# One stage for rotation, local attention and the decays of linear attention

## The chip, the core and the metric

The kernel runs on one core of a Trainium2 chip. The metric is the device time of one execution in microseconds. The core has TensorE (PE, matmuls into PSUM), VectorE (DVE), ScalarE (ACT), GpSimd (POOL) and SyncE (SP, here only the issue of DMAs); each has its own queue of instructions, and they wait for each other on semaphores. Everything is float32.

## What is computed

The reference is a trunk of two layers over 512 latent and 256 context tokens (768 rows, T) of width 1024. Layer 0 has a gated linear attention (GLA, 4 heads) beside a local attention (8 query heads, 2 key heads, window 128), layer 1 a latent attention; each layer ends in a mixture of 64 experts. Of layer 0 this matters:

```python
def apply_rope(x, ang):
    cos, sin = jnp.cos(a), jnp.sin(a)
    x1, x2 = xf[..., :half], xf[..., half:]
    return jnp.concatenate([x1 * cos - x2 * sin, x2 * cos + x1 * sin], axis=-1)

def gla_log_decay(a_low, wa2, ba):
    return jax.nn.log_sigmoid((a_low @ wa2 + ba).astype(jnp.float32)) / GLA_TAU
...
    cum = jnp.cumsum(ac, axis=2)                      # of the log decays, in a chunk
    o = einsum(qc * jnp.exp(cum), state) + ...
    state = jnp.exp(last)[..., None] * state + einsum(kc * jnp.exp(last - cum), vc)
...
    a_l = swa_latent(apply_rope(lsq, ang), apply_rope(lsk, ang), lsv, csk, csv, sink)
```

Latent queries and keys of the local attention are rotated, those of the context are not. A latent block of 128 queries sees all 256 context keys and the latent blocks beside it; a context block sees the context alone.

## The kernel before

Layer 0 is a row of stages (class `Phase`), each with its own buffers and semaphores and closed by a barrier of all engines. In order: `norm_transpose`, `even_project` (projections, with the modulation weights streamed through `wm` buffers), `rotate` (line 847), `window_attention` (line 894), `gla_decays` (line 516), `gla_states` (line 650), `gla_outputs`, `mix_out`, and the experts. Nothing reorders instructions: each engine runs its part of a stage as the code is written.

`rotate` turns six 128 x 512 tiles (four of queries `sqT`, two of keys `skT`). PE multiplies a tile by the constant `swap` (L871), DVE multiplies the result by the sines (L887), POOL the tile itself by the cosines (L878), DVE adds them (L891).

`window_attention` goes over six query tiles t of 128 rows (0 and 1 are context) and eight heads. PE writes the scores of one head to one of two `raw` buffers (L957 context keys, L959 near keys); DVE adds the mask and takes the maximum (L1017); after eight heads `maxima` gives the bias (L1023 to L1027); ACT takes the exponentials (L1072, L1076). PE turns them in quads of four heads and one key block (L969), DVE and ACT copy the even and the odd quads to `pT` (L1034, L1085), PE multiplies with the values (L981), ACT copies the result (L1091), PE turns it back (L991), DVE divides (L1039 to L1046). A loop over `steps(t)` (8, 8, 10, 12, 12 and 10 steps) pairs the scores of head i of tile t + 1 with quad i - 2 of tile t, the same on PE and DVE. Keys per tile: 2, 2, 4, 5, 5, 4 blocks, so scores are 256 wide for tiles 0 and 1, 512 for 2, 640 for 3 and 4, 512 for 5. "Tile t" below means step loop t, in which the scores of t + 1 are made.

`gla_decays` works on four 128 x 768 rows x of `qa` and `kb` (two directions, two pairs of heads). PE makes the logits in eight PSUM buffers (L551); ACT Abs (L628), Exp (L632), Ln (L635); DVE the other part of the log sigmoid (L567), the difference (L573), the cumulative sum (L575), the reversal for the backward direction (L580 to L586), the centring on the middle of each chunk (L590), the carries (L597, L602) and the scaled queries (L607); ACT the factors (L638, L640) and the carry factors (L646); POOL zeroes half of `qb` and `sm` (L614, L615) and multiplies the keys (L619). SP loads the small weights `wa` and `ba` once DVE has cleared `wa`.

`gla_states` issues the load of `w_out_e` (L1136), turns keys, and DVE runs the states from one chunk to the next. It does not wait for the zeroing within the stage.

## Time and profile before

| | us |
|---|---|
| median of 3 timed runs | 2854.18 |
| lowest, highest | 2849.14, 2856.47 |
| profiled execution | 2864.24 |
| its span, first to last instruction | 2861.7 |
| mean granted clock of PE | 0.930 |

The profile is one execution. Its times are from the span's start. "Busy" leaves out waiting; the granted clock is 1.00 at 2.4 GHz and 0.50 at 1.2 GHz. A bracket behind an instruction gives the engine's idle time before it and what ended it.

### The profile page before, as it was taken

The page shows a single profiled execution, that of the slowest core. Times are in us where ns is not written, and L with a number is a line of the kernel's source. Part 1 is how long each engine was busy: PE and PEld are TensorE (multiplying, and loading weights), DVE is VectorE, ACT ScalarE, POOL GpSimd, SP SyncE. Part 2 cuts the span into 40 slices and gives each one's busy share as a digit, 9 for nine tenths or more (in the row PEclk, how much of TensorE's full clock was granted, in tenths as well). Part 3 has the DMA queues.
Part 4 walks back from the last instruction along what each step waited for, and adds up shares of the span by engine and source line. Part 5 has one row for each costly group of instructions (what it writes and reads, how often), then busy time and mean ns, then how long its engine had stood idle before and what let it go on. Part 6 is the DMA issues. An engine that isn't in the chain of part 4 may idle for free. (4 is left out here: it accounts for less than half of the span.)

```text
span 2861.7 us, 30812 instructions
## 1 busy us (share of the span) xinstructions
PE 2522.1 (88%) x9117; PEld 1161.8 (41%) x9118; DVE 1200.0 (42%) x2435; ACT 410.1 (14%) x867; POOL 857.6 (30%) x1012
## 2 busy tenths in 40 slices
PE   6999794595599999999995998999389999999996
PEld 2665352452333333333332543554233333333332
DVE  2997255724633233332349112332533233332327
ACT  2000144221000000000014111222000000000002
POOL 0111102101354545545413001000054545545432
PEclk8999796797799999999998997999689999999998
DMA  7756000210599999999965201001479988998866
GB/s 255 226 191 220 19 1 1 65 67 32 223 369 365 361 348 361 350 364 364 363 266 228 66 30 67 1 1 44 178 252 355 345 324 331 338 337 336 331 221 272
DMA packets 163887, 634.31 MB, mean 222 GB/s; under 512 B 51710, under 2 KB 58282, under 8 KB 113506
## 3 DMA queue, kind: packets, MB, share of 16 engines
q10 hardware_dynamic: 59984, 389.57, 36.8%
q0 software_dynamic: 55280, 129.67, 12.4%
q1 hardware_dynamic: 48548, 114.13, 10.7%
q8 instruction: 39, 0.64, 0.1%
q14 instruction: 36, 0.29, 0.0%
HBM read 609.96 MB, written 74.58 MB: 239 GB/s over the span
## 5 line engine op out<-in xcount | busy, mean ns | idle before, releaser
L1759 POOL DMA_INDIRECT xg<-rows_x,p_idx x520 | 530.6, 1020 | 231.9 <-issue 122.0
L1847 PE MATMUL p_gu<-ring,p_xT 128*128 128x512 f32 x1024 | 455.7, 598 | 26.4 <-DVE p_xT L2088 26.4
L1859 PE MATMUL p_gu<-ring,p_xT 128*64 x1024 | 453.2, 595 | 0.0
L1860 PE MATMUL p_gu<-ring,p_xT 128*64 128x512 f32 x1024 | 453.1, 595 | 0.0
L2094 DVE TENSOR_TENSOR p_hid<-p_gu,p_sg 128x256 f32<-128x256 f32 x128 | 54.4, 425 | 580.8 <-ACT p_sg L1972 580.8
L1847 PEld LDWEIGHTS p_gu<-ring,p_xT 128*128 128x128 f32 x1024 | 192.0, 193 | 244.5 <-issue 244.5
L2088 DVE STREAM_TRANSPOSE p_xT<-xg 128x1024 f32<-128x1024 f32 x130 | 263.7, 2028 | 28.8 <-DMA xg<-rows_x,p_idx 27.1
L1859 PEld LDWEIGHTS p_gu<-ring,p_xT 128*64 128x64 f32 x1024 | 135.0, 137 | 263.9 <-issue 256.2
L2104 DVE COPY p_ys<-p_y 128x512 f32<-128x512 f32 x128 | 88.5, 692 | 365.6 <-PE p_y L1888 184.8
L1886 PE MATMUL p_y<-ring,p_hT 128*64 x512 | 233.4, 599 | 5.1 <-issue 5.1
L1875 PE MATMUL p_y<-ring,p_hT 128*128 128x512 f32 x512 | 236.9, 606 | 0.0
L1888 PE MATMUL p_y<-ring,p_hT 128*64 128x512 f32 x512 | 233.4, 598 | 0.0
L1972 ACT ACTIVATE p_sg<-p_gu 128x256 f32<-128x256 f32 x128 | 49.0, 383 | 877.9 <-PE p_gu L1860 439.6
L1773 POOL DMA_INDIRECT rows_y<-p_ys,p_y_idx x128 | 132.1, 1032 | 112.8 <-POOL p_y_idx L1770 111.9
L1875 PEld LDWEIGHTS p_y<-ring,p_hT 128*128 128x128 f32 x512 | 92.0, 189 | 143.8 <-issue 143.8
L1978 ACT COPY p_ys<-p_y 128x512 f32<-128x512 f32 x128 | 74.9, 585 | 424.6 <-PE p_y L1875 211.8
L1860 PEld LDWEIGHTS p_gu<-ring,p_xT 128*64 128x64 f32 x1024 | 135.0, 137 | 0.0
L1300 POOL TENSOR_TENSOR p_row<-p_tmp,p_mod_b 128x1024 f32<-128x1024 f32 x10 | 23.5, 2348 | 367.8 <-DVE p_tmp L1285 367.8
L1886 PEld LDWEIGHTS p_y<-ring,p_hT 128*64 128x64 f32 x512 | 64.8, 136 | 162.0 <-issue 162.0
L1770 POOL COPY p_y_idx<-slot_pair 128x1 int32 (+1 forms) x128 | 23.9, 186 | 348.5 <-DVE p_ys L2104 317.6
L453 PE MATMUL p_bank<-uT_e,w_in_e 128*128 128x384 f32 (+1 forms) x352 | 121.1, 500 | 2.3 <-PEq L111 2.3
L484 DVE SCALAR_TENSOR_TENSOR p_part<-p_wm,silu_c,p_part 128x256 f32<-128x256 f32 x273 | 111.3, 478 | 0.0
(424 smaller groups left out, 3066.8 us busy)
## 6 DMA issues: line engine op xcount, KB each, us to landing
ring<-in_w_exp_gate ACTq DMA_DIRECT2D x120, 1024.0 KB
ring<-in_w_exp_up ACTq DMA_DIRECT2D x120, 1024.0 KB
ring<-in_w_exp_down ACTq DMA_DIRECT2D x120, 1024.0 KB
ring<-rows_y SPq DMA_DIRECT2D x80, 512.0 KB, 12.8
p_wm<-in_w_mod POOLq DMA_DIRECT2D x24, 1024.0 KB
cat_e<-in_w_mod POOLq DMA_DIRECT2D x16, 1024.0 KB, 6.2
xg<-rows_x,p_idx POOLq DMA_INDIRECT x520
p_wmod<-in_w_mod SPq DMA_DIRECT2D x4, 2048.0 KB, 19.7
```

What stands on the lines that cost most here:

```text
L453: mm = nc.tensor.matmul(o, lhs, rhs, start=(k == 0), stop=(k == KD - 1))
L484: ins = nc.vector.scalar_tensor_tensor(acc, wm[sl % MBUF][:, k, :], c, acc, ALU.mult, ALU.add)
L1759: nc.gpsimd.indirect_dma_start(out=xg[q][:, part * D // QUADS:(part + 1) * D // QUADS], out_offset=None, in_=tr.rows_x[:, :].rearrange("t ...
L1773: nc.gpsimd.indirect_dma_start(out=tr.rows_y[:, :], out_offset=bass.IndirectOffsetOnAxis(ap=y_idx[q][:, 0:1], axis=0), in_=ys[q][:], in_of ...
L1847: mm = nc.tensor.matmul(gu[q][:], xT[q][:, k, :], w[:, :, k, :], start=(k == 0), stop=(k == KD - 1))
L1859: nc.tensor.matmul(gu[q][lower, :], xT[q][:, k, lower], wa[:, :, k, :], start=first, stop=last)
L1860: mm = nc.tensor.matmul(gu[q][upper, :], xT[q][:, k, upper], wb[:, :, k, :], start=first, stop=last)
L1875: mm = nc.tensor.matmul(yb[half], hT[q][:, k, :], w[:, k, half * 512:(half + 1) * 512], start=(k == 0), stop=(k == 1))
L1886: nc.tensor.matmul(yb[half][lower, :], hT[q][:, k, lower], wa[:, k, cols], start=(k == 0), stop=(k == 1))
L1888: mm = nc.tensor.matmul(yb[half][upper, :], hT[q][:, k, upper], wb[:, k, cols], start=(k == 0), stop=(k == 1))
L2088: nc.vector.transpose(xT[q][:].rearrange("p k (q b) -> p q k b", q=QUADS), xg[q][:].rearrange("p (q f k) -> p q k f", q=QUADS, k=KD)).then ...
L2104: nc.vector.tensor_copy(ys[q][:, 0:512], yb[0]).then_inc(y_v, 1)
```

## The change

Three stages become one, `local_attention`. `rotate` stays for layer 1 only, `gla_decays` is gone, its buffers `qa`, `kb` and `carry` are allocated earlier and lent to `even_project` as `wm` buffers. The context tiles need no rotation: the scores of tile 0 are made first, then come the six swaps and the four pairs of logits on PE, which uses the PSUM buffers of attention (`turn`, `ot`, `op` for the swaps, the two `raw` for the logits, each in turn). Abs and the splits follow them on ACT and DVE. Exp and Ln of the decays stand in ACT's queue after tile 0, differences and cumulative sums in DVE's steps 2 and 5 of tiles 1 and 2, the reversal and the centring in tile 3, the carries in tile 4, the scaled queries in tile 5; the factors stand in ACT's queue after tiles 3 and 4. The zeroing of `qb` and `sm` moves to `gla_states`.

```diff
         product, read_dve, read_act = ph.sem("product"), ph.sem("read_dve"), ph.sem("read_act")
-        wm = [ph.sb(f"wm{i}", [P, KD, MC])[:] for i in range(MBUF - 2)]
+        wm = [decays[:, i * KD * MC:(i + 1) * KD * MC].rearrange("p (k n) -> p k n", n=MC) for i in range(MBUF - 2)]
         wm += [spare[:, 2 * i:2 * i + 2, :].rearrange("p t (k n) -> p (t k) n", n=MC) for i in range(2)]
...
-def gla_decays(tr, qkT, aT, qa, kb, carry, qb, sm):
...
-    with Phase(nc) as ph:
-        wa = ph.sb("wa", [2 * GRANK, 2, GH * GDK])
-        ba = ph.sb("ba", [P, 4])
-        reset = ph.sb("reset", [P, T])
-        mid, total = ph.sb("mid", [P, 4, NT]), ph.sb("total", [P, 4, NT])
-        low = [ph.ps(f"low{i}", [P, 512]) for i in range(8)]
...
@@ -661,6 +527,13 @@
             @block.sync
             def _(sp):
                 load_ahead(sp)
+            @block.gpsimd
+            def _(pool):
+                for i in range(2):
+                    other = slice((1 - i) * GDK, (2 - i) * GDK)
+                    nc.gpsimd.memset(qb[other, :, :, i, :], 0.0)
+                    nc.gpsimd.memset(sm[other, :, :, i, :], 0.0)
             @block.tensor
             def _(pe):
...
-def window_attention(tr, sqT, skT, sv, cat):
+def local_attention(tr, sqT, skT, sv, cat, qkT, aT, qa, kb, carry):
...
+        wa = cat[0:2 * GRANK, 4, 0:2 * GH * GDK].rearrange("p (d n) -> p d n", d=2)
+        rope, part = cat[:, 0:2, 0:NLAT], cat[:, 2:4, 0:NLAT]
+        swap, ba = ph.sb("swap", [P, P]), ph.sb("ba", [P, 4])
+        reset = pT[:, CT + 2].rearrange("p h n -> p (h n)")[:, 0:T]
+        mid, whole = ph.sb("mid", [P, 4, NT]), ph.sb("whole", [P, 4, NT])
+        swaps = [turn[0][:].rearrange("p i n -> p (i n)"), turn[1][:].rearrange("p i n -> p (i n)"),
+                 ot[:].rearrange("p i n -> p (i n)"), op[:].rearrange("p i g e -> p (i g e)")]
...
     def _(sp):
         sp.dma_start(mask[:], dr["c_band"]).then_inc(loaded, 16)
         sp.dma_start(sink[:], dr["swa_sink"].to_broadcast([P, SH])).then_inc(loaded, 16)
+        sp.dma_start(swap[:], dr["c_swap"]).then_inc(rope_loaded, 16)
+        sp.dma_start(rope, dr["c_rope"]).then_inc(rope_loaded, 16)
+        sp.wait_ge(cleared, 1)
+        for d in range(2):
+            sp.dma_start(wa[d * GRANK:(d + 1) * GRANK, d, :], dr["gla_wa2"][0, d]).then_inc(wa_loaded, 16)
+            sp.dma_start(ba[:, 2 * d:2 * d + 2], dr["gla_ba"][0, d].rearrange("(j p) -> p j", p=P),
+                         allow_slow_non_contiguous=True) \
+                .then_inc(wa_loaded, 16)
+    @block.gpsimd
+    def _(pool):
+        pool.wait_ge(rope_loaded, 32)
+        for n, x in enumerate(rotating):
+            pool.wait_ge(swapped, n + 1)
+            nc.gpsimd.tensor_tensor(x, x, rope[:, 0, :], ALU.mult).then_inc(cosines, 1)
+        for x in range(4):
+            pool.wait_ge(factor_k, x + 1)
+            nc.gpsimd.tensor_tensor(kb[:, x, :], kb[:, x, :], qkT[:, 2 + x % 2, :], ALU.mult)
...
             n = t * SH + head
             if n >= 2:
                 pe.wait_ge(masked, n - 1)
+            if t == 1 and head < 2:
+                pe.wait_ge(split, 6 + 2 * head)
+                pe.wait_ge(absed, 6 + 2 * head)
+            if t == CT and head == 0:
+                pe.wait_ge(rotated, len(rotating))
...
+        def swap_halves():
+            pe.wait_ge(rope_loaded, 32)
+            for n, x in enumerate(rotating):
+                if n >= 4:
+                    pe.wait_ge(sines, n - 3)
+                nc.tensor.matmul(swaps[n % 4], swap[:], x, start=True, stop=True).then_inc(swapped, 1)
+        def decay_logits(x):
+            if x >= 2:
+                pe.wait_ge(split, 2 * (x - 1))
+                pe.wait_ge(absed, 2 * (x - 1))
+            else:
+                pe.wait_ge(masked, SH - 1 + x)
+            for hf in range(2):
+                mm = nc.tensor.matmul(raw[x % 2][:, hf * 512:hf * 512 + HALF],
+                                      wa[:, x // 2, (x % 2) * P:(x % 2 + 1) * P],
+                                      aT[:, hf * HALF:(hf + 1) * HALF], start=True, stop=True)
+            mm.then_inc(logits, 1)
         def turn_quad(n):
             t, b, q = quads[n]
             pe.wait_ge(probs, SH * t + 4 * (q + 1))
-            if n >= 2:
+            if n < 2:
+                pe.wait_ge(sines, len(rotating))
+            else:
                 pe.wait_ge((placed_v, placed_a)[n % 2], n // 2)
...
         for head in range(SH):
             score(0, head)
+        swap_halves()
+        pe.wait_ge(wa_loaded, 64)
+        for x in range(4):
+            decay_logits(x)
...
     def _(dve):
+        nc.vector.memset(wa, 0.0).then_inc(cleared, 1)
+        nc.vector.memset(reset, 1.0).then_inc(cleared, 1)
+        dve.wait_ge(cleared, 2)
+        nc.vector.memset(reset[:, 0:T:P], 0.0).then_inc(cleared, 1)
         dve.wait_ge(loaded, 32)
+        def turn_halves():
+            dve.wait_ge(rope_loaded, 32)
+            for n, x in enumerate(rotating):
+                dve.wait_ge(swapped, n + 1)
+                if n >= 2:
+                    dve.wait_ge(rotated, n - 1)
+                nc.vector.tensor_tensor(part[:, n % 2, :], swaps[n % 4], rope[:, 1, :], ALU.mult) \
+                    .then_inc(sines, 1)
+                if n:
+                    add_cosines(n - 1)
+            add_cosines(len(rotating) - 1)
+        def add_cosines(n):
+            x = rotating[n]
+            dve.wait_ge(sines, n + 1)
+            dve.wait_ge(cosines, n + 1)
+            nc.vector.tensor_tensor(x, x, part[:, n % 2, :], ALU.add).then_inc(rotated, 1)
+        def split_logits(x):
+            dve.wait_ge(absed, 2 * x + 2)
+            for hf in range(2):
+                nc.vector.tensor_scalar(kb[:, x, hf * HALF:(hf + 1) * HALF], raw[x % 2][:, hf * 512:hf * 512 + HALF],
+                                        ba[:, x:x + 1], 0.0, ALU.add, ALU.min).then_inc(split, 1)
+        def sum_decays(x):
+            dve.wait_ge(logged, x + 1)
+            dve.wait_ge(split, 2 * x + 2)
+            nc.vector.tensor_tensor(kb[:, x, :], kb[:, x, :], qa[:, x, :], ALU.subtract).then_inc(decay, 1)
+            dve.wait_ge(decay, x + 1)
+            dve.wait_ge(cleared, 3)
+            nc.vector.tensor_tensor_scan(qa[:, x, :], reset, kb[:, x, :], 0.0, ALU.mult, ALU.add) \
+                .then_inc(cum_done, 1)
+        def turn_round():
+            dve.wait_ge(cum_done, 4)
+            nc.vector.tensor_copy(whole[:], cum[:, :, :, P - 1]).then_inc(mids, 1)
+            nc.vector.tensor_copy(mid[:, 0:2, :], cum[:, 0:2, :, MID]).then_inc(mids, 1)
+            nc.vector.tensor_tensor(kb[:, 2:4, :], kb[:, 2:4, :], qa[:, 2:4, :], ALU.subtract) \
+                .then_inc(relative, 1)
+            dve.wait_ge(relative, 1)
+            nc.vector.tensor_copy(mid[:, 2:4, :], rel[:, 2:4, :, MID]).then_inc(mids, 1)
+        def centre(x):
+            dve.wait_ge(mids, 3)
+            src = cum if x < 2 else rel
+            nc.vector.tensor_tensor(rel[:, x], src[:, x], mid[:, x, :].unsqueeze(2).to_broadcast([P, NT, P]),
+                                    ALU.subtract).then_inc(relative, 1)
+        def sum_carry(d, s):
+            a, b = ORDER[d][s], ORDER[d][s + 1]
+            xs = slice(2 * d, 2 * d + 2)
+            nc.vector.tensor_tensor(carry[:, d, b, :], mid[:, xs, b], mid[:, xs, a], ALU.subtract) \
+                .then_inc(carried, 1)
+            dve.wait_ge(carried, 2 * (2 * s + d) + 1)
+            tot = a if d == 0 else b
+            nc.vector.tensor_tensor(carry[:, d, b, :], carry[:, d, b, :], whole[:, xs, tot], ALU.add) \
+                .then_inc(carried, 1)
+        def scale_queries(x):
+            dve.wait_ge(factor_q, x + 1)
+            nc.vector.scalar_tensor_tensor(qa[:, x, :], qkT[:, x % 2, :], float(GDK ** -0.5), qa[:, x, :],
+                                           ALU.mult, ALU.mult)
+        def decays_between(t, i):
+            if 1 <= t < CT + 1 and i in (2, 5):
+                sum_decays(2 * (t - 1) + (i == 5))
+            if t == 3 and i == 1:
+                turn_round()
+            if t == 3 and 3 <= i < 7:
+                centre(i - 3)
+            if t == 4 and i % 2 == 0 and i < 10:
+                for d in range(2):
+                    sum_carry(d, i // 2)
+            if t == 5 and i % 2 == 1 and i < 8:
+                scale_queries(i // 2)
...
@@ -1051,6 +1072,9 @@
         for head in range(SH):
             mask_scores(0, head)
         maxima(0)
+        turn_halves()
+        for x in range(4):
+            split_logits(x)
         for t in range(NT):
             for i, (head, quad) in enumerate(steps(t)):
                 if head is not None:
@@ -1061,6 +1085,7 @@
                     place(quad)
                 if t and i == BACK:
                     norm(t - 1)
+                decays_between(t, i)
         norm(NT - 1)
     @block.scalar
...
@@ -1084,6 +1109,20 @@
                     act.wait_ge(turned, n + 1)
                     nc.scalar.copy(pT[:, b, 4 * q:4 * q + 4, :], turn[1][:]).then_inc(placed_a, 1)
+        def log_decays():
+            for x in range(4):
+                act.wait_ge(absed, 2 * x + 2)
+                nc.scalar.activation(qa[:, x, :], qa[:, x, :], ACT.Exp, scale=-1.0).then_inc(exped, 1)
+            for x in range(4):
+                act.wait_ge(exped, x + 1)
+                nc.scalar.activation(qa[:, x, :], qa[:, x, :], ACT.Ln, bias=tr.ones[:, 0:1]).then_inc(logged, 1)
+        def factors(x):
+            act.wait_ge(relative, x + 2)
+            nc.scalar.activation(qa[:, x, :], kb[:, x, :], ACT.Exp, scale=1.0 / GTAU).then_inc(factor_q, 1)
+            act.wait_ge(factor_q, x + 1)
+            nc.scalar.activation(kb[:, x, :], kb[:, x, :], ACT.Exp, scale=-1.0 / GTAU).then_inc(factor_k, 1)
         def place_o(t):
             act.wait_ge(attended, t + 1)
             if t:
@@ -1091,11 +1130,28 @@
             nc.scalar.copy(oT[:], ot[:]).then_inc(o_placed, 1)
         exps(0)
+        act.wait_ge(wa_loaded, 64)
+        for x in range(4):
+            act.wait_ge(logits, x + 1)
+            for hf in range(2):
+                nc.scalar.activation(qa[:, x, hf * HALF:(hf + 1) * HALF], raw[x % 2][:, hf * 512:hf * 512 + HALF],
+                                     ACT.Abs, bias=ba[:, x:x + 1]).then_inc(absed, 1)
         for t in range(NT):
             place(t)
             if t + 1 < NT:
                 exps(t + 1)
             place_o(t)
+            if t == 0:
+                log_decays()
+            if t in (3, 4):
+                for x in (2 * t - 6, 2 * t - 5):
+                    factors(x)
+        act.wait_ge(carried, 4 * (NT - 1))
+        for d in range(2):
+            b = ORDER[d][0]
+            for lo, hi in ((0, b), (b + 1, NT)):
+                if lo < hi:
+                    nc.scalar.activation(carry[:, d, lo:hi, :], carry[:, d, lo:hi, :], ACT.Exp, scale=1.0 / GTAU)
 def even_mixer(tr, layer):
@@ -1108,6 +1164,8 @@
 with ExitStack() as st:
     early, aT = sb("early", [P, 3, NT * GH * GDV]), sb("aT", [2 * GRANK, T])
+    decays, carry = sb("decays", [P, 2 * 4 * T]), sb("carry", [P, 2, NT, 2])
+    qa, kb = (decays[:, i * 4 * T:(i + 1) * 4 * T].rearrange("p (x t) -> p x t", x=4) for i in range(2))
     qkT = early[:, 0, :].rearrange("p (x t) -> p x t", x=4)
     v, gs = (early[:, i, :].rearrange("p (t n) -> p t n", t=NT) for i in (1, 2))
     with ExitStack() as st:
@@ -1122,17 +1180,13 @@
                     load_group(sp, tr, w, w_loaded, g)
             norm_transpose(tr, layer, uT, load_ahead)
-            even_project(tr, uT, qkT, aT, sqT, skT, v, gs, sv, cat, w, w_loaded)
-        rotate(tr, [sqT[:, i, NCTX:T] for i in range(SH // 2)] + [skT[:, i, NCTX:T] for i in range(SKV)])
-        window_attention(tr, sqT, skT, sv, cat)
+            even_project(tr, uT, qkT, aT, sqT, skT, v, gs, sv, cat, decays, w, w_loaded)
+        local_attention(tr, sqT, skT, sv, cat, qkT, aT, qa, kb, carry)
     with ExitStack() as late:
         w_out = late.enter_context(nc.sbuf_tensor("w_out_e", [P, KD, D], F32))
         out_loaded = nc.alloc_semaphore("w_out_e_loaded")
         with ExitStack() as st:
-            qa, kb = sb("qa", [P, 4, T]), sb("kb", [P, 4, T])
-            carry, sm = sb("carry", [P, 2, NT, 2]), sb("sm", [P, NT, 4, 2, GDV])
-            qb = sb("qb", [P, 4, NT, 2, P])
-            gla_decays(tr, qkT, aT, qa, kb, carry, qb, sm)
+            sm, qb = sb("sm", [P, NT, 4, 2, GDV]), sb("qb", [P, 4, NT, 2, P])
             gla_states(tr, early[:, 0, :], qa, qb, kb, v, carry, sm, lambda sp: sp.dma_start(
                 w_out[:], tr.dram["w_out_e"][0].rearrange("(p k) n -> p k n", k=KD)).then_inc(out_loaded, 16))
             gla_outputs(tr, early[:, 0, :], qa, qb, kb, v, sm, gs, cat)
```

DVE, between the maxima of tile 0 and the first masks of the scores of tile 1 (`p_raw` are scores or logits, `decays` is `qa` and `kb`, `cat_e` lends its rows to rope, sines and part). Before:

```order
L1023 SCALAR_TENSOR_TENSOR p_m<-p_top,p_sink 128x8
L1026 TENSOR_SCALAR p_nm<-p_m 128x8
L1027 TENSOR_TENSOR p_ed<-p_sink,p_m 128x8
L1017 ISA p_s,p_top<-p_raw,p_mask 128x256
L1017 ISA p_top 128x1
```

Now:

```order
L1048 TENSOR_TENSOR p_ed<-p_sink,p_m 128x8
L960 TENSOR_TENSOR cat_e<-p_turn,cat_e 128x512 x2
L971 TENSOR_TENSOR sqT<-sqT,cat_e 128x512
L960 TENSOR_TENSOR cat_e<-p_ot,cat_e 128x512
L971 TENSOR_TENSOR sqT<-sqT,cat_e 128x512
L960 TENSOR_TENSOR cat_e<-p_op,cat_e 128x512
L971 TENSOR_TENSOR sqT<-sqT,cat_e 128x512
L960 TENSOR_TENSOR cat_e<-p_turn,cat_e 128x512
L971 TENSOR_TENSOR sqT<-sqT,cat_e 128x512
L960 TENSOR_TENSOR cat_e<-p_turn,cat_e 128x512
L971 TENSOR_TENSOR skT<-skT,cat_e 128x512 x2
L976 TENSOR_SCALAR decays<-p_raw,p_ba 128x384 x8
```

Twelve operations of the rotation and eight splits now stand ahead of the masks that follow.

ACT, from the exponentials of the scores made in tile 0 to those made in tile 1. Before:

```order
L1072 ACTIVATE p_s,p_total<-p_s,p_nm 128x256 x8
L1076 ACTIVATE p_es<-p_ed 128x8
L1091 COPY p_oT<-p_ot 128x512
L1085 COPY p_pT<-p_turn 128x512 x2
L1072 ACTIVATE p_s,p_total<-p_s,p_nm 128x512 x8
```

Now:

```order
L1097 ACTIVATE p_s,p_total<-p_s,p_nm 128x256 x8
L1101 ACTIVATE p_es<-p_ed 128x8
L1130 COPY p_oT<-p_ot 128x512
L1115 ACTIVATE decays<-decays 128x768 x4
L1118 ACT_TABLE_LOAD
L1118 ACTIVATE decays<-decays,ones 128x768 x4
L1110 COPY p_pT<-p_turn 128x512 x2
L1097 ACT_TABLE_LOAD
L1097 ACTIVATE p_s,p_total<-p_s,p_nm 128x512 x8
```

Eight activations and two loads of a table now stand around the two copies of tile 1's quads.

## Rows read from the trace of the kernel before

**Rows 1.** the stage borders in the timeline: start us, length us, engine, line, operation

```profile
315.53 0.35 SPq L862 DMA_DIRECT2D p_rope<-in_c_rope  x1
333.65 0.33 SPq L944 DMA_DIRECT2D p_mask<-in_c_band  x1
...
453.11 2.65 POOL L614 MEMSET qb<- 64x3072 f32 x1 [122.03 <-POOLq L111]
...
503.82 0.34 SPq L1136 DMA_DIRECT2D w_out_e<-in_w_out_e  x1
```

**Rows 2.** windows by query tile: length, busy us (x count) per engine, granted clock, DMA

```profile
343.25:358.52 15.27, 15.09 (x40) 6.96 (x40) 5.78 (x26) 7.60 (x28) 0.00 (x0) 0.50 0.00 1
358.52:370.41 11.89, 11.11 (x62) 6.68 (x60) 8.15 (x25) 3.51 (x13) 0.00 (x0) 1.00 0.01 1
370.41:390.14 19.73, 17.65 (x86) 9.79 (x84) 10.44 (x28) 12.21 (x31) 0.00 (x0) 1.00 0.00 0
390.14:412.18 22.04, 19.77 (x98) 10.97 (x96) 11.12 (x28) 10.85 (x26) 0.00 (x0) 1.00 0.00 1
412.18:439.67 27.49, 25.94 (x99) 15.86 (x97) 10.37 (x28) 9.99 (x26) 0.00 (x0) 0.69 0.00 1
416.70:433.70 17.00, 17.00 (x53) 11.36 (x52) 7.02 (x20) 2.34 (x4) 0.00 (x0) 0.50 0.00 1
439.67:452.33 12.66, 9.17 (x58) 5.50 (x56) 4.73 (x12) 4.49 (x11) 0.00 (x0) 1.00 0.00 1
```

**Rows 3.** three rows of attention's timeline, one each of DVE, PE and ACT

```profile
344.50 0.42 DVE L1017 CUSTOM_DVE_ANT_0 p_s<-p_raw,p_mask 128x256 f32<-128x256 f32 x1 [0.48 <-PE p_raw L957]
...
354.91 3.68 PE L981 MATMUL p_ot<-p_pT,sv 128*64 128x512 f32 x8
...
360.28 0.56 ACT L1091 COPY p_oT<-p_ot 128x512 f32<-128x512 f32 x1
```

**Rows 4.** rotation stage, by line (busy us, mean ns, idle before); a window; DVE's timeline

```profile
L871 PE MATMUL p_bank<-sqT,p_swap 128*128 128x512 f32 x8 | 6.2, 949 | 5.6 <-DMA p_swap<-in_c_swap 5.6
...
318.00:321.00 3.00, 1.67 (x2) 0.84 (x3) 0.00 (x0) 0.00 (x0) 0.00 (x0) 0.50 0.19 70
...
321.52 0.69 DVE L887 TENSOR_TENSOR p_part<-p_bank,p_rope 128x512 f32<-128x512 f32 x1 [14.33 <-PE p_bank L871]
...
332.26 0.69 DVE L891 TENSOR_TENSOR skT<-skT,p_part 128x512 f32<-128x512 f32 x1
```

**Rows 5.** the decays' stage, grouped by line

```profile
L551 PE MATMUL p_low<-aT,p_wa 32*128 32x384 f32 x16 | 10.6, 852 | 5.8 <-DMA p_ba<-in_gla_ba 5.8
L575 DVE TENSOR_TENSOR_SCAN qa<-p_reset,kb 128x768 f32<-128x768 f32 x4 | 7.0, 1757 | 0.1
L602 DVE TENSOR_TENSOR carry<-carry,p_total 128x2 f32<-128x2 f32 x10 | 6.2, 617 | 0.3
...
L567 DVE TENSOR_SCALAR kb<-p_low,p_ba 128x384 f32<-128x384 f32 x8 | 4.6, 613 | 10.9 <-ACT qa L628 10.9
L628 ACT ACTIVATE qa<-p_low,p_ba 128x384 f32<-128x384 f32 x8 | 4.2, 576 | 14.0 <-PE p_low L551 14.0
L573 DVE TENSOR_TENSOR kb<-kb,qa 128x768 f32<-128x768 f32 x4 | 3.8, 939 | 4.1 <-ACT qa L635 4.1
...
L635 ACT ACTIVATE qa<-qa,ones 128x768 f32<-128x768 f32 x4 | 3.4, 922 | 0.0
...
L632 ACT ACTIVATE qa<-qa 128x768 f32<-128x768 f32 x4 | 3.0, 838 | 0.0
...
L635 ACT ACT_TABLE_LOAD x1 | 1.3, 1283 | 0.0
```

**Rows 6.** tile 4's slow spell, timeline of DVE, then of PE

```profile
420.08 0.69 DVE L1017 CUSTOM_DVE_ANT_0 p_s<-p_raw,p_mask 128x512 f32<-128x512 f32 x1 [2.35 <-PE p_raw L959]
...
423.13 0.69 DVE L1017 CUSTOM_DVE_ANT_0 p_s<-p_raw,p_mask 128x512 f32<-128x512 f32 x1 [1.24 <-PE p_raw L959]
...
429.97 4.48 PE L969 MATMUL p_turn<-ident,p_s 128*128 128x128 f32 x20
```

More of the change, by code:

```diff
@@ L345, in load_group, with even_project @@
         eng.dma_start(w[g % 2][:, :, 0:b - a], w_dram[:, :, a:b]).then_inc(w_loaded[g % 2], 16)
-def even_project(tr, uT, qkT, aT, sqT, skT, v, gs, sv, spare, w, w_loaded):
+def even_project(tr, uT, qkT, aT, sqT, skT, v, gs, sv, spare, decays, w, w_loaded):
     nc, dr = tr.nc, tr.dram
@@ L891, in _ @@
                     nc.vector.tensor_tensor(x, x, part[:, n % 2, :], ALU.add).then_inc(rotated, 1)
-def window_attention(tr, sqT, skT, sv, cat):
+def local_attention(tr, sqT, skT, sv, cat, qkT, aT, qa, kb, carry):
     nc, dr = tr.nc, tr.dram
     NK = NCTX + 3 * P
+    HALF = T // 2
     scale = float(SHD ** -0.5)
+    rotating = [sqT[:, i, NCTX:T] for i in range(SH // 2)] + [skT[:, i, NCTX:T] for i in range(SKV)]
     def keys(t):
```

123 lines of the change are left out of this document (9 added, 114 removed).

## Prediction

> **What bounds the kernel now.** I began with the stage borders [rows 1]. The change touches only 315.53 to 503.82 us of the span: the rotation stage (315.53 to 333.65), local attention (333.65 to 453.11) and the decays (453.11 to 503.82). Each stage ends in a barrier of all engines, so an engine that is idle in one stage cannot start on the next. Whatever these 188 us shrink by, all that follows starts earlier by the same amount: the weights of the experts are loaded in later stages, and the load of w_out_e is issued when the stage of the states opens [rows 1], before and after the change.
>
> Next I read the windows by query tile of attention [rows 2]. The reader is to see three things. TensorE (PE) is busy 11.11 of 11.89 us in tile 1, 17.65 of 19.73 in tile 2 and 19.77 of 22.04 in tile 3, so it bounds the middle tiles. VectorE (DVE) is busy about half of the time there, ScalarE (ACT) between 30 and 62%: this is the cover that the change wants for the decays. And the granted clock is 0.50 (1.2 GHz) in tile 0, 1.00 (2.4 GHz) in tiles 1 to 3, and 0.50 again for 17 us inside tile 4, where PE is busy the whole time. So PE's clock, not only its idle time, sets the length of a tile.
>
> **What is removed.** The rotation stage is 333.65 - 315.53 = 18.1 us, the decays' stage 503.82 - 453.11 = 50.7 us [rows 1]. Together 68.8 us. All their work comes back inside attention, except the zeroing of qb and sm, which GpSimd (POOL) now does in the stage of the states. There the four memsets (2.65 us each, 10.6 in all [rows 1]) stand first on POOL's queue and nobody waits for them but the end of that stage; DVE and ACT work there for far longer on other rows. Cost nothing; if that cover were gone, 10.6 us.
>
> **What is inserted between tile 0 and tile 1 of the scores.** In the old order DVE takes the first mask of tile 1 at 344.50 [rows 3]. Now PE, DVE and ACT first do the rotation and the decays' logits, and DVE has them all in front of that mask. (a) Rotation: DVE's chain ran from 321.52 to 332.95 [rows 4], 11.4 us for six products and six sums. Issuing a product ahead of each sum saves a little; I take 11.0, starting at about 345.4, one matmul after the maxima, to 356.4. (b) Splits of the first two logits: 8 operations are 4.6 us [rows 5], so 1.15 a pair: 358.7. Their matmuls and Abs were done beside the rotation. (c) Logits now share two PSUM buffers instead of eight, so the third waits for the first split (357.5): 4 matmul passes at 10.6/16 = 0.66 [rows 5] are 2.65, Abs 1.15, split 1.15: 362.5. The fourth queues behind it on PE: 362.85, Abs 364.0, split 365.1. The mask of tile 1 comes at 365.1 instead of 344.50: +20.6. At 2.4 GHz the logits would take half, +17.5; if the six sums met POOL as the carries do, whose mean of 617 ns for two elements is waiting [rows 5], some +23. I take +20.5. The stage's loads cost nothing: mask and sink are still first on SP's queue, rope and swap are wanted 10 us later. Three short DVE memsets lie under that load's wait.
>
> **Tile 1.** After tile 0's output copy, which ended at 360.84 in old time [rows 3], ACT has four Exp (3.03), a table load (1.28) and four Ln (3.41) [rows 5] queued ahead of the copies of turned probabilities. DVE, in its third step of that tile, waits for the first Ln: 360.84 + 3.03 + 1.28 + 0.92 = 366.1, then a difference 0.94 and a scan 1.76 [rows 5]: 368.8, and only then masks the fourth score. PE has two score buffers and stops at the sixth score, due at about 365.4, until 369.4. So PE idles 4 us. A second difference and scan (2.7) holds the seventh mask back, and the first score of tile 2 waits for it. If PE keeps 2.4 GHz the tile grows by 5.8 us. The second table load falls into ACT's wait for the maxima, cost nothing (1.3 without).
>
> But I do not expect it to keep the clock. Where PE waited 5.6 us for the swap matrix it came back at a granted clock of 0.50 [rows 4], and the 17 us spell of tile 4 began without a gap of even 4 us (PE is idle 1.5 us in the whole tile [rows 2]). A slow step of one 512-wide score and one turned quad is 3.05 us (420.08 to 423.13 [rows 6]); the quad alone is 4.48/5 = 0.9, taken as 1.0, so the score is 2.0. From 369.4 at 1.2 GHz: three scores 6.0, one quad and one turn back 2.0, values 3.7 [rows 3]: 381.1 instead of 370.41. Tile 1: +10.8, or +13 if slow from its start; the inserted work is hidden then.
>
> **Tile 2.** Wider scores at 1.2 GHz: 2.0 plus 2 x (0.66 - 0.51) = 2.3. Eight of them, eight quads and a turn back: 18.4 + 9 = 27.4. The values are 16 passes, 7.3 us at 1.2 GHz by the eight of [rows 3]; such a run brought the clock up at the end of tile 0, so I take half of it at either level, 5.5. Together 32.9 instead of 19.73: +13.2. Two more differences and scans are hidden under the slow PE. At 2.4 GHz they are not: they hold back the last two masks and the placing of the quads, and the tile would grow by 2.8.
>
> **Tiles 3 to 5.** Tile 3 has the turn round (1.9 by the 768-wide difference doubled, plus three small copies, say 2.3) and four centrings as wide as that difference, 0.94 each: 6.1 us on a DVE that is busy 11.12 of 22.04. Up to the middle PE's two buffers absorb it; the last mask and the placing of the last quads come 3 us late, +3. Tile 4 has 20 small carry operations: ten of them took 6.2 us with POOL at work [rows 5], DVE is free 17 us there [rows 2], and ACT's first four factors (as wide as the Exp, 4 x 0.84 = 3.4 [rows 5]) fall into an idle stretch: between 0 and +3, I take +0.5. In tile 5 ACT is on the path with PE; four factors stand ahead of its copies: +3.4. The three small carry exponentials run beside the last turn back.
>
> **The sum.** 20.5 + 10.8 + 13.2 + 3 + 0.5 + 3.4 = 51.4 added, 68.8 removed: 17.4 us shorter. The profiled execution had a span of 2861.7 us (2864.2 with what lies around it); the median of the three timed runs is 2854.2, and I take the same difference from it: 2836.8.
>
> On what lifts the clock, the trace has PE doing 20 transposes back to back, with no other matmul, when the slow spell of tile 4 ends at about 433.7 [rows 2, 6]. The Trainium skill says otherwise ("TensorE: Matmul & The Clock Gate", section "Part 4: PE-mode transpose"): transposes do not count as PE activity for the clock gate. By that rule the quads that close tiles 2 to 4 could never lift the clock and only the values could, about 1 us later per tile; by the row they can. The measurement decides, and the sum stands without this paragraph.
>
> **Rivals.** *B, the clock goes as it did* (low in tile 0, high in 1 to 3): 20.5 + 5.8 + 2.8 + 3 + 0.5 + 3.4 = 36.0, 32.8 shorter, 2821. For it: values of tile 1 may bring the clock up again as those of tile 0 did. Against: the 4 us gap. If the slow spell of tile 4 also went, some 7 more. *C, low clock to the end of tile 3's scores*: 20.5 + 13 + 15 + 14.6 + 0.5 + 3.4 = 67, 2 shorter, 2852. For it: tile 0 was slow for 15 us with PE busy 15.09 of them, and nothing but values or bare transposes is seen to end such a spell. *D, slower:* the clock stays at 1.2 GHz from the insertion to the stage's end. Tiles 1 to 5 would take 24.7, 34.7, 38.6, 36.2 and 18, against 11.9, 19.7, 22.0, 27.5 and 12.7: +58.4, with the insertion and part of the last factors +81, so 12 slower, 2866. It decides from about 40 us of further slow PE time. Against it: runs of values get longer (16 to 20 passes) in tiles 2 to 4, and shorter ones ended the spell of tile 0. *E, the change does not do what it says:* the decays' operations sit in DVE's order in such a way that every one is exposed. That is 10.8 of differences and scans, 6.1 of turn round and centrings, some 6.2 of carries and 3.8 of query products, 27 in all; with the insertion and ACT's 3.4 it still leaves 18 shorter. It is within A's range and gets no chance of its own.
>
> **How the numbers follow.** Forecast A 45%, B 33%, C 14%, D 8%. The likeliest is A, 2836.8. A alone has the bounds of its terms, 2829 to 2844. For 8 times in 10 the range must take in B with its own spread and most of C: 2815 to 2855. About 0.3% (8.6 us) is what a measurement can tell from no change. Faster by more: nearly all of A and B, 0.77. Within: C and the edge of A, 0.15. Slower by more: D, 0.08.
>
> **What would show it.** In the profile after, the stage that opens near 315.5 should end near 486 (A) or 471 (B) with the states' first DMA; the first 256-wide mask of tile 1 comes 20 us later against the stage's start than before. ACT shows four Exp, load, four Ln in a row, and DVE idles about 3 us in front of the first difference. PE shows a gap of 4 us in tile 1, and the clock row tells A from B: 0.50 or 1.00 in the 30 us after it. I am wrong if the insertion is much off 20 us (the chain of two PSUM buffers), if the clock does not fall after the gap, or if any stage behind attention changes length.

## The result, and the profile after

Interleaved on one chip, the kernel after took 2833.03 us (median of 4 runs, 2830.35 to 2835.04), the kernel before 2855.32 (4 runs): ratio 0.9926, 95% interval 0.9908 to 0.9943, so 22 us faster. The forecast was 2836.8. The profiled execution of the kernel after took 2830.35 us with a span of 2827.6, against 2864.24 and 2861.7 before.

The stage borders of the kernel after in the timeline (start us, length us, engine, line, operation), which answer to [rows 1]:

```profile
315.44 0.35 SPq L835 DMA_DIRECT2D p_mask<-in_c_band  x1
...
471.94 2.65 POOL L535 MEMSET qb<- 64x3072 f32 x1 [14.87 <-POOLq L111]
...
471.94 0.34 SPq L1190 DMA_DIRECT2D w_out_e<-in_w_out_e  x1
```

The merged stage is 156.5 us where the three were 188.3: 31.8 shorter, not 17.4. The windows of the kernel after, from the stage's start to the first mask of tile 1's scores, then by query tile, each to the end of its values (the last to the stage's end); columns as in [rows 2]:

```profile
315.44:346.74 31.30, 21.27 (x46) 9.95 (x46) 18.77 (x43) 9.63 (x26) 9.20 (x6) 0.70 0.14 42
346.74:359.64 12.90, 12.72 (x40) 6.36 (x40) 5.06 (x22) 2.35 (x7) 0.00 (x0) 0.55 0.00 0
359.64:380.14 20.50, 14.58 (x63) 8.62 (x61) 12.51 (x25) 13.40 (x26) 0.00 (x0) 0.75 0.00 1
380.14:404.44 24.30, 20.95 (x88) 11.27 (x86) 16.09 (x36) 14.24 (x37) 0.00 (x0) 0.86 0.00 1
404.44:429.44 25.00, 21.20 (x99) 11.24 (x98) 16.09 (x36) 10.53 (x24) 0.00 (x0) 0.93 0.00 0
429.44:450.14 20.70, 18.31 (x98) 10.94 (x96) 14.51 (x49) 11.46 (x26) 3.62 (x2) 1.00 0.00 1
450.14:471.94 21.80, 14.02 (x58) 8.37 (x56) 7.33 (x15) 7.95 (x18) 3.57 (x2) 0.69 0.00 1
```

Cut in the same way, the kernel before has 10.85 us to that mask, then 14.1, 11.9, 19.7, 22.0 and 27.5, and 10.4 to the last values (18.6 now). Against its clocks [rows 2], the slow spell of tile 4 is gone; tiles 1 to 3 and 5 have short ones that were not there.

**Insertion.** DVE's first product of the rotation, its last two sums, and the first mask of tile 1's scores:

```profile
327.57 0.69 DVE L960 TENSOR_TENSOR cat_e<-p_turn,cat_e 128x512 f32<-128x512 f32 x1 [1.17 <-PE p_turn L882]
...
336.40 1.56 DVE L971 TENSOR_TENSOR skT<-skT,cat_e 128x512 f32<-128x512 f32 x2
...
346.74 0.41 DVE L1038 CUSTOM_DVE_ANT_0 p_s<-p_raw,p_mask 128x256 f32<-128x256 f32 x1
```

**Tile 1.** ACT's queue after tile 0 and what waits for it on DVE and PE:

```profile
362.97 3.04 ACT L1115 ACTIVATE decays<-decays 128x768 f32<-128x768 f32 x4
366.02 1.28 ACT L1118 ACT_TABLE_LOAD   x1
367.32 3.41 ACT L1118 ACTIVATE decays<-decays,ones 128x768 f32<-128x768 f32 x4
...
368.29 0.96 DVE L982 TENSOR_TENSOR decays<-decays 128x768 f32<-128x768 f32 x1 [4.24 <-ACT decays L1118]
...
371.68 1.22 PE L871 MATMUL p_raw<-skT,sqT 64*128 64x256 f32 x2 [5.14 <-DVE p_top L1038]
```

The chain is the one forecast: Ln, difference, scan, mask, score. PE idles 5.14 us (4 forecast). The clock over it, in windows (the third column from the end):

```profile
364.00:366.00 2.00, 2.00 (x11) 1.20 (x10) 0.05 (x1) 2.00 (x3) 0.00 (x0) 1.00 0.00 0
...
368.00:370.00 2.00, 0.00 (x0) 0.00 (x0) 1.68 (x2) 2.00 (x4) 0.00 (x0) 0.67 0.00 0
370.00:372.00 2.00, 0.32 (x1) 0.32 (x2) 2.00 (x4) 1.20 (x2) 0.00 (x0) 0.50 0.00 0
372.00:376.00 4.00, 4.00 (x14) 2.83 (x15) 2.06 (x8) 1.09 (x2) 0.00 (x0) 0.50 0.02 4
376.00:380.00 4.00, 4.00 (x16) 1.46 (x14) 3.97 (x7) 0.78 (x1) 0.00 (x0) 0.64 0.00 0
380.00:381.00 1.00, 1.00 (x9) 0.85 (x8) 0.78 (x5) 0.18 (x1) 0.00 (x0) 1.00 0.00 0
```

It falls in the gap, as forecast, but is back at 1.00 by the end of tile 1's values (377.6 to 380.2) and does not stay low through tile 2. There it falls once more, behind a wait of PE of 1.37 us, and is back within the values of that tile, at about 403:

```profile
393.00:396.00 3.00, 1.77 (x8) 0.93 (x8) 3.00 (x5) 0.58 (x1) 0.00 (x0) 1.00 0.01 3
396.00:399.00 3.00, 2.09 (x10) 1.75 (x12) 1.83 (x6) 0.83 (x2) 0.00 (x0) 0.50 0.00 0
399.00:402.00 3.00, 3.00 (x8) 0.96 (x10) 0.00 (x0) 3.00 (x9) 0.00 (x0) 0.50 0.02 5
402.00:405.00 3.00, 3.00 (x16) 1.18 (x14) 0.00 (x0) 3.00 (x8) 0.00 (x0) 0.87 0.00 0
```

**Tile 5** has the same pattern, which was not forecast. ACT's last two factors, the copy behind them, PE's wait for it, and the windows over it:

```profile
453.34 0.83 ACT L1122 ACTIVATE decays<-decays 128x768 f32<-128x768 f32 x1
454.20 0.84 ACT L1124 ACTIVATE decays<-decays 128x768 f32<-128x768 f32 x1
454.95 0.57 ACT L1110 COPY p_pT<-p_turn 128x512 f32<-128x512 f32 x1
...
455.66 1.09 PE L904 MATMUL p_turn<-ident,p_s 128*128 128x128 f32 x4 [3.28 <-ACT p_pT L1110]
```

```profile
450.00:456.00 6.00, 2.21 (x16) 1.65 (x15) 2.52 (x5) 5.45 (x11) 2.49 (x2) 0.83 0.00 0
456.00:465.00 9.00, 7.46 (x30) 5.34 (x30) 4.06 (x8) 1.75 (x3) 1.08 (x1) 0.50 0.01 2
```

**Behind attention** one stage changed. The first 6 us of the states' stage, in the kernel before and in the kernel after:

```profile
503.82:510.00 6.18, 6.13 (x46) 5.00 (x47) 0.00 (x0) 1.75 (x3) 0.00 (x0) 0.60 0.92 341
...
471.94:478.00 6.06, 5.78 (x68) 4.68 (x68) 0.00 (x0) 2.24 (x4) 6.02 (x3) 1.00 0.91 347
```

Before, PE had idled 36 us in the decays' stage and got through 46 matmuls in that stretch, at a clock of 0.60; now it comes from attention after 1.81 us of waiting and gets through 68, at 2.4 GHz. The stage is 26.7 us instead of 28.7. Coming straight from attention does not ensure it: in the run `early_logs` below, with the same code here and the same wait of 1.81 us, the first 6 us ran at 0.50 and the stage took 29.2. With the 0.1 us by which the projections ended sooner, and under half a microsecond of other differences, that makes the 34.1 us between the spans.

### The profile page after: what moved, and what is told of

Read it like the earlier page. It is cut to its first block and busy times, and to the rows that moved or that the text cites. A ratio compares the mean times of both kernels' runs of the same rounds, so it can differ in the third digit from the quotient of the medians.

```text
span 2827.6 us, 30777 instructions
## 1 busy us (share of the span) xinstructions
PE 2521.5 (89%) x9117; PEld 1161.6 (41%) x9118; DVE 1192.4 (42%) x2435; ACT 409.8 (14%) x867; POOL 855.6 (30%) x1012
## 3 DMA queue, kind: packets, MB, share of 16 engines
q1 hardware_dynamic: 48676, 114.13, 10.8%
## 5 line engine op out<-in xcount | busy, mean ns | idle before, releaser
L1824 POOL COPY p_y_idx<-slot_pair 128x1 int32 (+1 forms) x128 | 23.6, 184 | 349.3 <-DVE p_ys L2158 330.6
L484 DVE SCALAR_TENSOR_TENSOR p_part<-decays,silu_c,p_part 128x256 f32<-128x256 f32 x273 | 111.1, 476 | 0.0
## 6 DMA issues: line engine op xcount, KB each, us to landing
ring<-rows_y SPq DMA_DIRECT2D x80, 512.0 KB, 12.8
```

What stands on the lines that cost most here:

```text
L484: ins = nc.vector.scalar_tensor_tensor(acc, wm[sl % MBUF][:, k, :], c, acc, ALU.mult, ALU.add)
```

## Experiments

Each run was compared with the kernel before on its own chip. The runs named `again_` and `only_` shared one chip, `early_logs` to `all_three` a second, the rest a third. "Stage" is the time from the first load of the rotation or attention to that of `w_out_e`, in the one profiled execution; tile lengths are cut as above.

**Both kernels again.**

> The kernel before, profiled once more, to see what the 9 us are by which its first profile (2864 us) lay above its timed runs (2855). Theory S (the clock of attention varies): the stage of attention, 119.5 us in the first profile, comes out 5 to 12 us shorter whenever no slow-clock spell falls into tile 4, and every other stage keeps its length within 1 us. Rival E (another stage varies): attention is 119.5 us again and the difference, if there is one, sits in the experts (886 and 848 us) or the projections. Ratio to the kernel before 1.000.

> The changed kernel, profiled once more. Theory S: its merged stage is 156.5 us in the first profile; with other positions of the slow spells it may be 150 to 170, all other stages as before within 1 us. Rival E: 156.5 again and the total differs elsewhere. Ratio to the kernel before 0.992 to 0.993 either way.

The kernel before gave 188.1 us of stage and tiles of 14.1, 11.9, 19.7, 22.0, 27.4 and 10.4; the kernel after 157.3 us and 13.1, 20.5, 24.3, 25.1, 20.9 and 18.6: every tile within 0.2 us of its first profile, clocks and slow spells included. The ratios: 1.0012 (0.9984 to 1.0040) and 0.9898 (0.9867 to 0.9929).

So of the two theories on record the rival, E, held in the main: attention keeps its length, and the difference sits elsewhere. The first profile of the kernel before was 8.8 us of span longer than this one, and the merged stages make 0.2 us of it: 6.9 lie in layer 1 ahead of its experts (447.3 and 440.4 us) and 1.7 in its experts (848.0 and 846.3), which the change does not touch. In the same untouched parts the kernel after varies too, 446.9 and 442.3 us ahead of the experts. In the timed runs on that chip the kernel before took from 2843.7 us, at a mean clock of 0.936, to 2868.7, at 0.928.

**One part alone.** The kernel before with the rotation in attention (first diff, with POOL's products as in the kernel after); the kernel after with `rotate` as a stage of its own and the swaps, products and sums taken out of attention (second):

```diff
+                    if t == CT and head == 0:
+                        pe.wait_ge(rotated, len(rotating))
...
                 for head in range(SH):
                     score(0, head)
+                swap_halves()
...
                 maxima(0)
+                turn_halves()
```

```diff
+        rotate(tr, [sqT[:, i, NCTX:T] for i in range(SH // 2)] + [skT[:, i, NCTX:T] for i in range(SKV)])
         local_attention(tr, sqT, skT, sv, cat, qkT, aT, qa, kb, carry)
...
-                swap_halves()
...
-                turn_halves()
```

> Only the rotation goes into the attention stage (swaps, sines, sums between tile 0's maxima and tile 1's scores); the decays stay a stage of their own. Removed 18.1 us of stage; DVE's chain of 11.5 us in the changed kernel (326.4 to 337.9) comes back in front of tile 1's masks. Theory of additive parts: 6.6 us shorter, ratio 0.9977. Rival (the barrier and the loads of the rotation stage were hidden anyway, or the inserted work changes the clock of tiles 0 and 1): within 2 us of nothing, or over 12 shorter.

> Only the decays go into the attention stage; the rotation stays a stage of its own. Removed 50.7 us; the logits' chain over two PSUM buffers without the rotation's cover inserts 11.6 us, and tiles 1 to 5 grow as in the changed kernel, by 25 us against a kernel before without slow spell. Theory of additive parts: 14 us shorter, ratio 0.995. Rival (the two parts share their cover): more than 17 or less than 10 shorter, so that the parts' gains don't add to the 22 us of both.

Rotation alone: stage 183.0, ratio 0.9963 (0.9943 to 0.9982), the inserted work 11.9 us, all tiles as in the kernel before, the spell of tile 4 among them. Decays alone: stage 177.4, ratio 0.9938 (0.9914 to 0.9963), the inserted work 13.5. Its tiles 1, 3 and 4 (the windows of this kernel):

```profile
371.67:392.15 20.48, 14.49 (x63) 8.59 (x61) 12.45 (x25) 13.43 (x26) 0.00 (x0) 0.75 0.00 1
...
413.69:444.43 30.74, 29.05 (x99) 16.15 (x98) 16.75 (x36) 10.85 (x26) 0.00 (x0) 0.67 0.00 0
444.43:471.87 27.44, 25.88 (x97) 15.84 (x98) 16.48 (x49) 13.15 (x30) 3.58 (x2) 0.69 0.00 1
```

Tile 1 is the kernel after's to 0.02 us: it belongs to the decays. But tiles 3 and 4, with the same instructions as in the kernel after, take 30.7 and 27.4 us against 25.0 and 20.7, with PE busy nearly throughout: slow spells. So in the profiles the parts do not add: 5.3 + 10.9 = 16.2 us of stage against 31.8 together. Some 12 of the 15.6 us between them are these two spells. The timed runs of the same chip say otherwise: 0.9963 x 0.9938 = 0.9901, against 0.9898 for both parts together. The profiled execution of the decays alone was the slowest of its six (2852.4 us, median 2844.7), so its two spells need not be typical. By time the parts add within the noise; that they do not is not shown.

**Three edits to take off the exposed work.** Exp and Ln of the decays ahead of tile 0's copies on ACT (`early_logs`); four PSUM buffers for the logits instead of two (`four_buffers`); two of the four last factors after each of two copies of tile 4 (`factors_tile4`):

```diff
+                    if x in (1, 3):
+                        exp_decays((x - 1, x))
+                ln_decays()
                 for t in range(NT):
                     place(t)
...
-                    if t == 0:
-                        log_decays()
```

```diff
+        lows = [[raw[x][:, hf * 512:hf * 512 + HALF] for hf in range(2)] for x in range(2)]
+        lows += [[swaps[i][:, 0:HALF] for i in pair] for pair in ((2, 3), (0, 1))]
...
-                        nc.tensor.matmul(raw[x % 2][:, hf * 512:hf * 512 + HALF],
+                        nc.tensor.matmul(lows[x][hf],
```

```diff
                             nc.scalar.copy(pT[:, b, 4 * q:4 * q + 4, :], turn[1][:]).then_inc(placed_a, 1)
+                            if t == 4 and n - before(t) in (1, 3):
+                                factors(2 + (n - before(t)) // 2)
```

> The changed kernel with ScalarE's four Exp, the table load and four Ln of the decays moved ahead of tile 0's loop, into the idle time that the logits' chain leaves there. Theory (ScalarE's queue makes the gap of tile 1): PE's 5.1 us gap in tile 1 goes, tile 1 falls from 20.5 us to 14 to 16, with the clock at 1.00 through it; the merged stage from 156.5 to about 151. Rival (VectorE's two sums make it): tile 1 stays above 18 us.

> The changed kernel with the third and fourth logits in the banks of turn, ot and op, free once the sines are read, instead of in the two score buffers a second time. Theory (the chain over two buffers is serial time): the first mask of tile 1 comes 4.4 us earlier, 27 us after the stage's start instead of 31.3, and the stage is 4 to 5 shorter if the clock behaves the same. Rival (the rotation's DVE work alone sets it): under 2 us earlier.

> The changed kernel with the last four factors of ScalarE between its copies in tile 4, where it idles 3 us at a time, instead of ahead of tile 5's copies. Theory (tile 5 grew by 8.3 us, 3.4 of ScalarE's work and 5 because PE's 3.3 us gap brought its clock down): tile 5 from the end of the fourth values to the states' first DMA falls from 21.7 to about 13.5, clock 1.00 in it. Rival (it grew by VectorE's query products): 18 or more.

> The three edits together. If they add: stage 156.5 - 5.8 - 4.4 - 8 = 138 us, 18 shorter than the changed kernel, ratio to the kernel before about 0.983. If the slow spells only move to other tiles, as they did when the decays alone were merged: 145 to 155 us, and the tile that has the spell shows a mean clock near 0.67 with PE busy all through.

| | stage us | to the mask | tiles 0 to 5 | ratio (95%) |
|---|---|---|---|---|
| kernel after | 156.5 | 31.3 | 12.9 20.5 24.3 25.0 20.7 18.6 | 0.9926 (0.9908-0.9943) |
| early_logs | 164.0 | 31.8 | 13.2 12.8 31.8 25.1 27.4 18.9 | 0.9893 (0.9862-0.9924) |
| four_buffers | 149.6 | 26.8 | 13.5 18.8 22.5 25.1 20.9 18.8 | 0.9872 (0.9841-0.9902) |
| factors_tile4 | 154.1 | 31.7 | 13.0 20.5 24.3 25.0 23.6 12.9 | 0.9889 (0.9858-0.9919) |
| all_three | 160.4 | 26.8 | 13.7 12.7 33.2 30.7 28.9 11.2 | 0.9896 (0.9876-0.9917) |

Each edit did its own job: 7.7 us off tile 1, 4.5 off the insertion, 5.7 off tile 5. But `early_logs` lost all of it and more in tiles 2 and 4, and `all_three`, at 160.4 us, is slower in the stage than the kernel after, and slower than both outcomes on record. The ratios do not rank these runs: their intervals overlap one another and that of the kernel after on the repeated pair's chip (0.9867 to 0.9929). What the edits did is read from one profile each. Windows of `early_logs` over its tile 2, and the end of that spell on PE:

```profile
374.00:375.50 1.50, 1.19 (x4) 0.57 (x3) 1.50 (x4) 1.50 (x5) 0.00 (x0) 0.71 0.00 0
375.50:397.50 22.00, 21.95 (x56) 12.43 (x54) 13.48 (x28) 6.08 (x17) 0.00 (x0) 0.50 0.00 0
397.50:398.50 1.00, 0.80 (x4) 0.72 (x4) 0.69 (x1) 0.06 (x1) 0.00 (x0) 0.50 0.03 8
398.50:399.50 1.00, 0.22 (x3) 0.04 (x1) 0.00 (x0) 0.69 (x2) 0.00 (x0) 0.99 0.00 0
```

```profile
395.49 1.97 PE L904 MATMUL p_turn<-ident,p_s 128*128 128x128 f32 x8
397.70 1.01 PE L904 MATMUL p_turn<-ident,p_s 128*128 128x128 f32 x4 [0.25 <-ACT p_pT L1110]
399.50 1.08 PE L916 MATMUL p_ot<-p_pT,sv 128*64 128x512 f32 x4 [0.78 <-issue]
```

For 22 us PE is busy 21.95 at 1.2 GHz: keeping it busy does not bring its clock back. (The fall itself, at about 374.6, came 2 us behind a wait of 1.23.) The spell ends after twelve transposes in a row, ahead of the values, as that of tile 4 did before. The Trainium skill says that the full clock does not engage for transposes, which do not count as PE-busy in the same way ("TensorE: Matmul & The Clock Gate", "Part 4: PE-mode transpose"); these two rises speak against it, though the scores ran until 395.5 and a late effect of theirs is not excluded.

**The gap filled.** Five unused matmuls in the gap of tile 1, on PE ahead of that tile's sixth step:

```diff
+                        if t == 1 and i == 5:
+                            for _ in range(5):
+                                nc.tensor.matmul(swaps[3], swap[:], rotating[0], start=True, stop=True)
```

> The kernel after, with five extra matmuls of 128 rows and 512 columns (result unused, into op's bank, which is free there) on PE ahead of the sixth step of tile 1, where PE idles 5.1 us and the granted clock falls from 0.94 to 0.50. At 2.4 GHz they are about 0.86 us each, 4.3 in all, so nearly hidden by the gap. Theory 1 (the idle gap brings the clock down): the clock stays at 1.00 in tile 1, which shrinks from 20.5 us to about 18, and tile 2 loses nothing; the stage is 154 us instead of 156.5. Theory 2 (the clock falls whenever PE does mostly scores and transposes for some time, gap or none): the fall only comes later, in tile 2, and tile 1 + tile 2 together stay near 45 us or grow.

PE in the gap, then the windows of tiles 1 and 2 in this kernel:

```profile
366.59 4.46 PE L939 MATMUL p_op<-sqT,p_swap 128*128 128x512 f32 x10
371.51 0.70 PE L871 MATMUL p_raw<-skT,sqT 64*128 64x256 f32 x2 [0.46 <-DVE p_top L1041]
```

```profile
359.89:376.60 16.71, 15.46 (x72) 8.41 (x70) 10.96 (x22) 12.97 (x24) 0.00 (x0) 1.00 0.00 1
376.60:408.62 32.02, 29.08 (x86) 15.56 (x86) 17.89 (x39) 14.22 (x36) 0.00 (x0) 0.63 0.00 1
```

The first half of theory 1 holds: with the wait nearly as long as before (4.92 us) but filled, the clock stays at 1.00 and tile 1 is 3.8 us shorter. `early_logs`, which has no such wait, has 1.00 through tile 1 as well. So the idle gap brought the clock down. But tile 2 now takes 32.0 us instead of 24.3: the stage is 161.4, as theory 2 had it. Ratio 0.9918 (0.9895 to 0.9942).

**Matmuls added to the kernel before.**

```diff
+                        if t == 3 and i == 2:
+                            pe.wait_ge(normed, t - 1)
+                            for _ in range(3):
+                                nc.tensor.matmul(op[:].rearrange("p i g e -> p (i g e)"), tr.ident[:], sv[:, 0:4, :],
+                                                 start=True, stop=True)
```

> The kernel before, with three extra matmuls of 128 rows and 512 columns (result unused, into op's bank) on PE ahead of the third step of tile 3's loop (the one that scores tile 4), about 414 us. They cost 3 x 0.86 = 2.6 us, less the 0.78 us that PE waits there. Before, PE then stays at a granted clock of 0.50 for 17 us though it is never idle, and the tile takes 27.5 us. Theory 1 (the mix of work ahead of 417 us decides, values and other matmuls of 128 rows keep the clock up): the spell goes, the tile takes 27.5 - 7 + 1.8, about 22 us, the attention stage 5 us less. Theory 2 (idle time of 0.8 us is what starts the spell): with the wait filled the spell also goes. Theory 3 (the spell comes when these scores and transposes have run for some time, whatever stands ahead): it stays or only starts later, the tile takes 24 to 29 us.

The place on record is wrong: by the trace they run at 392.6, in tile 3, over 20 us ahead of where the spell of tile 4 began, not at 414. This is PE there, and the window of tile 4:

```profile
392.60 2.84 PE L1001 MATMUL p_op<-sv,ident 128*128 128x512 f32 x6
```

```profile
415.21:435.62 20.41, 18.21 (x98) 10.97 (x98) 10.19 (x28) 9.99 (x26) 0.00 (x0) 1.00 0.00 1
```

Tile 3 grew by 1.8 us, and yet tile 4 took 20.4 instead of 27.5 with the clock at 1.00 throughout. The stage is 184.5 instead of 188.3; the time, 0.9990 (0.9973 to 1.0007), cannot tell that from nothing. The run shows that tile 4's own instructions alone do not bring the spell. It cannot tell whether the added work or the shift in time did it.

**Two edits, and two with the gap filled.** `four_buffers` with `factors_tile4`:

> The kernel after with two edits: the decays' logits in four PSUM buffers instead of two, and the first four factors of ACT moved from the start of tile 5 into tile 4. Alone they gave a stage of 149.6 and 154.1 us against 156.5. If the slow spells stay where they are with four buffers (tiles 1 and, in part, 3), the gains add: stage about 147 us, span near 2818, ratio to the kernel before about 0.986. If the factors of ACT in tile 4 bring a slow spell there, as in the run with them alone (tile 4 +3.4), they still give 2.4: 147. Rival: another spell appears in tiles 2 to 4, as with all three edits: stage 153 or more.

> The two edits and the five extra matmuls in tile 1's gap. If the idle gap is what brings the clock down in tile 1: tile 1 goes from 18.8 to about 17 us and the stage is 1 to 2 us shorter than with the two edits alone. If not, the spell moves to tile 2 (22.5 us with a clock of 1.00 in the run with four buffers) and the stage is longer by 5 us or more.

Stage 157.3 and 157.5 us, against 147 on record for the gains adding and 153 or more for the rival; ratios 0.9876 (0.9850 to 0.9902) and 0.9896 (0.9865 to 0.9926). `two_edits` and `four_buffers` have the same instructions on every engine to the end of tile 3. Tiles 2 and 3 of `four_buffers`:

```profile
374.49:396.99 22.50, 18.41 (x86) 10.29 (x84) 17.16 (x39) 12.16 (x31) 0.00 (x0) 1.00 0.00 0
396.99:422.09 25.10, 21.30 (x98) 11.49 (x96) 16.09 (x36) 12.57 (x30) 0.00 (x0) 0.93 0.00 1
```

and of `two_edits`:

```profile
377.00:400.79 23.79, 20.04 (x86) 10.68 (x86) 16.72 (x38) 13.90 (x35) 0.00 (x0) 0.93 0.00 1
400.79:431.51 30.72, 29.03 (x98) 16.15 (x98) 16.71 (x36) 9.27 (x22) 0.00 (x0) 0.67 0.00 0
```

The same code gave 25.1 us in one execution and 30.7 in another, on another chip. So a single profile does not settle these small edits: a difference of 7 us in the stage may be where a spell fell. `two_edits` itself was timed at 2821.4, 2823.2 and 2827.5 us beside its profiled 2832.1. Filling the gap brought tile 1 from 18.8 to 16.3 us and its clock to 1.00, and again tile 2 was slow: 31.8 us. Yet the stage grew by 0.2 us only, since tile 3 then took 23.4 at 1.00 instead of 30.7; neither outcome on record was that.

One pattern holds in all ten profiles that have the decays in attention. In the four where the clock stayed up in tile 1, tile 2 took 31.8 to 33.2 us; in the six where a gap had brought it down there, 21.5 to 24.3.

## Why the prediction was right in size and wrong in its terms

The sum was 68.8 removed, 51.4 added. Measured in the profiles: 68.8 removed, 37.0 added.

| step | forecast | measured |
|---|---|---|
| insertion ahead of tile 1's first mask | +20.5 | +20.45 |
| tile 0 | 0 | -1.1 |
| tile 1 | +10.8 | +8.6 |
| tile 2 | +13.2 | +4.6 |
| tile 3 | +3 | +3.0 |
| tile 4 | +0.5 | -6.8 |
| tile 5 and the end | +3.4 | +8.4 |

So the number was right by luck. The signs named ahead tell A from B, and they point more to B: the clock fell in the gap, as in A, but was low for 13 of the 30 us behind it only, and the stage ended at 471.94, as in B (471) and not as in A (486). B's sum, 36.0 added, is near the 37.0 measured, but also by errors that offset: it has neither the -6.8 of tile 4 nor 5 of the 8.4 us of tile 5.

*Insertion: right*, link by link. DVE shows the first product at 12.1 us after the stage's start (11.75 forecast), the end of the last sum at 22.5 (22.75) and the mask at 31.3 (31.45). With four buffers it is 4.5 us shorter: the wait of the third logits for the split was real.

*Tile 1: the mechanism was right*, shown by `fill_gap` and by `early_logs`, which removes the wait (12.8 us). The gap was 5.1 instead of 4 us, but the clock came back in the values.

*Tile 2: the step that failed.* "Stays low until values of tile 2" priced a whole tile at 1.2 GHz, 8.6 us too much. The argument given for B, that the values of tile 1 may lift the clock as those of tile 0 did, was the right one. The clock was then low for 7 us only, from 396 to about 403.

*Tile 3: the size was right*; its clock of 0.93 was not in the sum, so the 3 us are partly that.

*Tile 4: missed.* I kept the slow spell where it was, and named its going only as a mishap of rival B ("some 7 more"). It went: -6.8.

*Tile 5: the work was priced, its consequence was not.* The four factors take 3.3 us on ACT; PE's idle 3.28 us then brought the clock down, as in tile 1, and turns and values ran at 1.2 GHz until about 467.6 us. With these factors moved forward tile 5 is 12.9 us instead of 18.6, at a price of 2.9 in tile 4.

*Covers.* The second table load and the zeroing in the states' stage cost nothing, as forecast (the first load was priced in the chain of tile 1). The stage's own loads cost 0.6 us: the first mask of tile 0, which waits for the load of the sinks in both kernels, comes 4.5 us after the stage's start instead of 3.9. The claim that nothing behind attention changes length was wrong by 2.0 us in our favour.

*Slips of the sum.* 381.1 instead of 370.41 is 10.7 us, not 10.8. E priced ten carry operations, 6.2 us; the other ten took 3.1 in the kernel before, so E would leave 15 us shorter, not 18.

The forecast lay 3.8 us from the median, for two reasons that offset each other. The terms gave 14 us too little gain. And I carried a difference of spans over to the medians: the profiled execution before was 8.9 us above its median of 2855.32, the one after 2.7 below its own, so 33.9 us between the profiled executions are 22.3 between the medians (about 16 to 26 by the interval). By the repeated pair, the 8.9 us lie in parts that the change does not touch. In stage length that pair again differs by 30.8 us; its spans differ by 26.7, since the untouched parts there went the other way, and its chip gave 29.2 by the ratio. Why the first comparison's medians show 22.3 and not the 34 of the merged stage and the states together stays open: its timed executions may have had their spells elsewhere, as those of `two_edits` may have, and only one of each is profiled.

What sets where a spell falls also stays open. Not tried: profiling one kernel many times with its start shifted.
